# Column sums of a modulation row: seven of twelve made by TensorE transpositions and VectorE row sums

## The reference, cut to what matters

```python
def modulation(cond, w, b, n):
    m = jax.nn.silu(cond) @ w[:, :n * D_MODEL] + b[:n * D_MODEL]
    return jnp.split(m, n, axis=-1)
...
sh, sc, gt = modulation(c_lat, w_ada[i], b_ada[i], 3)
u = x * (1.0 + sc) + sh
```

## Time and profile before

| | us |
|---|---|
| median of 3 runs (lowest, highest) | 1789.02 (1788.63, 1791.81) |
| the profiled execution's own time | 1790.88 |
| its span, first to last instruction | 1789.1 |
| mean granted TensorE clock, share of full speed | 0.990 |
| TensorE matmul busy | 1737.5 |
| VectorE busy | 1334.8 |
| ScalarE busy | 903.4 |

### The profile page before, as it was taken

How to read it: one execution, slowest core, us unless ns; L and a number is a source line. 1 busy time by engine, 2 the same in 40 slices (tenths; PEclk the granted TensorE clock), 3 DMA queues, 4 the chain that set the end, 5 groups by cost and what they waited for, 6 DMA issues and landing times.

```text
span 1789.1 us, 22330 instructions
## 1 busy us (share of the span) xinstructions
PE 1737.5 (97%) x8112; PEld 1396.1 (78%) x8112; DVE 1334.8 (75%) x1779; ACT 903.4 (50%) x1366; POOL 142.2 (8%) x202
## 2 busy tenths in 40 slices
PE   7999999999999999999999999999989989999997
PEld 6887887788877777888677778787767768777885
DVE  6967777868777777687876767788676878766766
ACT  7446563455456644464653456555633355443432
POOL 1100000001100000011111100000101101110000
PEclk9999999999999999999999999999999999999999
DMA  8955454558845544679877843333748879876563
GB/s 294 323 190 187 167 165 142 184 181 285 273 155 163 176 141 143 252 275 377 273 249 235 298 176 120 129 117 120 273 165 324 298 267 316 285 252 226 199 215 118
DMA packets 110406, 390.36 MB, mean 218 GB/s; under 512 B 16200, under 2 KB 16864, under 8 KB 108736
## 3 DMA queue, kind: packets, MB, share of 16 engines
q1 hardware_dynamic: 74672, 268.99, 42.6%
q0 software_dynamic: 27856, 101.19, 18.3%
q10 hardware_dynamic: 7776, 18.82, 2.8%
HBM read 384.75 MB, written 4.19 MB: 217 GB/s over the span
## 4 chain that ended last, share of the span: by engine, by line
PE 79%; DVE 11%; DMA 4%; ACT 3%; issue 3%; ACTq 0%; DVEq 0%; SPq 0%
PE L L329 22%; PE L L331 21%; PE L L330 21%; DVE wl L282 3%; PE TP L433 3%; DMA stage<-in_w_stream 2%; DVE macc L596 1%; DMA mstage<-in_w_mod 1%; PE AB L1872 1%; PE AB L1800 1%; ACT wh L261 1%; PE AB L1877 1%; PE AB L1876 1%; PE TP L1886 1%; PE AB L2102 1%
## 5 line engine op out<-in xcount | busy, mean ns | idle before, releaser
L329 PE MATMUL L<-wh,xth 128*128 128x512 f32 x1952 | 797.2, 408 | 15.2 <-DVE wl L282 8.6
L282 DVE TENSOR_TENSOR wl<-stage,wh 128x1024 fp32r<-128x1024 f32 x504 | 613.4, 1221 | 249.6 <-ACT wh L261 248.8
L261 ACT ACTIVATE wh<-stage 128x1024 fp32r<-128x1024 f32 x504 | 531.1, 1057 | 521.8 <-PE L L331 377.8
L331 PE MATMUL L<-wh,xtl 128*128 128x512 f32 x1952 | 767.5, 393 | 0.0
L330 PE MATMUL L<-wl,xth 128*128 128x512 f32 x1952 | 765.6, 392 | 0.0
L329 PEld LDWEIGHTS L<-wh,xth 128*128 128x128 f32 x1952 | 370.1, 190 | 113.3 <-issue 22.7
L331 PEld LDWEIGHTS L<-wh,xtl 128*128 128x128 f32 x1952 | 369.3, 189 | 80.9
L330 PEld LDWEIGHTS L<-wl,xth 128*128 128x128 f32 x1952 | 370.6, 190 | 75.3 <-issue 4.8
L596 DVE SCALAR_TENSOR_TENSOR macc<-mstage,scols,macc 128x1024 f32<-128x1024 f32 x240 | 306.9, 1279 | 11.3 <-DMA mstage<-in_w_mod 11.0
L625 POOL DMA_DIRECT2D mstage<-in_w_mod x192 | 139.2, 725 | 1499.0 <-DVE macc L596 1031.5
L1174 DVE SCALAR_TENSOR_TENSOR pa<-tab,AB 128x384 f32<-128x384 f32 x48 | 26.6, 555 | 65.3 <-PE AB L1872 35.1
(11 more groups left out here) (205 smaller groups left out, 1332.4 us busy)
## 6 DMA issues: line engine op xcount, KB each, us to landing
stage<-in_w_stream SPq DMA_DIRECT2D x504, 512.0 KB, 4.5
mstage<-in_w_mod POOLq DMA_DIRECT2D x192, 512.0 KB, 6.0
X<-in_x SPq DMA_DIRECT2D x4, 512.0 KB, 8.0
arena<-in_ctx ACTq DMA_DIRECT2D x1, 2048.0 KB, 14.2
x_kept<-X ACTq DMA_DIRECT2D x1, 2048.0 KB, 10.6
X<-x_kept ACTq DMA_DIRECT2D x1, 2048.0 KB, 8.3
arena<-in_b_ada ACTq DMA_DIRECT2D x2, 1024.0 KB, 10.6
arena<-in_ln_g ACTq DMA_DIRECT2D x2, 1024.0 KB, 9.0
```

What stands on the lines that cost most here:

```text
L261: nc.scalar.activation(wh[:, s % SPLITS].rearrange("p a b -> p (a b)"), stage[:, s % RING, :], ACT.Copy).then_inc(hi_ready, 1)
L282: nc.vector.tensor_tensor(wl[:, s % SPLITS].rearrange("p a b -> p (a b)"), stage[:, s % RING, :], wh[:, s % SPLITS].rearrange("p a b -> p ...
L329: nc.tensor.matmul(o, xh, w[0], start=start, stop=False, skip_group_check=True)
L331: last = nc.tensor.matmul(o, xl, w[0], start=False, stop=True, skip_group_check=True)
```

## The change

Seven of the twelve sums (i = 1 in both layers, two each, and i = 4, 5 and 6) are made in another way. TensorE transposes the eight pieces of `macc` into turning banks (`turn_sums`), four to a bank, so one sum takes two uses. VectorE sums each bank along its rows (`sum_turned`, 128 x 4 x 128 to 128 x 4) into a new small buffer `msum`, which frees the bank, and adds the bias as before (`mod_columns_turned`), now from `msum`; it raises `mod_summed` itself. The four uses per layer, named ("ms", l, j), stand in TURNS ahead of the next layer's x turns. In the layers, TensorE makes them in two groups of two uses behind slots 3 and 5 (before: all behind slot 5), and VectorE reads them in its steps 4 and 6, and adds the bias in step 6 (before: step 8). The sum for i = 4 stands behind slot 23 (before: 25) and its wait for `r_sb` falls away; VectorE's part is in its step 26 (before: 30). The sum for i = 5 stays, with its wait for `z_min` moved behind the loop. Waits for `mod_cols` in TensorE's list fall away. The counters of the uses are moved on in ScalarE's and TensorE's lists. The other five sums stay as they are.

```diff
-    return t + [("yb", l, 3)] + [("x", l + 1, m) for m in range(4)]
+    return t + [("yb", l, 3)] + [("ms", l, j) for j in range(4)] + [("x", l + 1, m) for m in range(4)]
...
+        msum = sb("msum", [P, 2, 8])
...
+        def flat_bank(m):
+            return TP[(m - 1) % 2].rearrange("p a b -> p (a b)")
...
+        def sum_turned(dve, m, w, j):
+            dve.wait_ge(tp_ready, m)
+            nc.vector.tensor_reduce(msum[:, w, 4 * j:4 * j + 4], flat_bank(m).rearrange("p (c k) -> p c k", c=4), AX.X, ALU.add)\
+                .then_inc(bank_free(m), 1)
+
+        def mod_columns_turned(dve, c, scale, targets, uses):
+            for m in uses:
+                turned(dve, m)
+            for w, which, layer in targets:
+                nc.vector.scalar_tensor_tensor(out=mcols[:, which, at(c, 8)], in0=msum[:, w, :],
+                                               scalar=1.0 if scale else 0.0,
+                                               in1=bcols[:, layer].rearrange("p a b -> p (a b)")[:, at(c, 8)],
+                                               op0=ALU.add, op1=ALU.add).then_inc(mod_cols, 1)
+            dve.sem_inc(mod_summed, 1)
...
(ScalarE)
+            u.n += 2
             evac_ctx = evac_to(0, 2048, 1024)
...
                     turned(act, u.n)
+                    u.n += 4
...
(VectorE, layer end)
-                    if n == 8:
-                        mod_columns(dve, 2 * l + 1, 8 * l + KT, True, [(0, 1, 0), (1, 0, 0)])
+                    if n in (4, 6):
+                        for j in range(2):
+                            sum_turned(dve, TURN["ms", l, n - 4 + j], n // 2 - 2, j)
+                    if n == 6:
+                        mod_columns_turned(dve, 8 * l + KT, True, [(0, 1, 0), (1, 0, 0)], [TURN["ms", l, j] for j in range(4)])
...
+            def mod_columns_block2(w, c, scale, which):
+                uses = [u.take()[1] for _ in range(2)]
+                for j, m in enumerate(uses):
+                    sum_turned(dve, m, w, j)
+                mod_columns_turned(dve, c, scale, [(w, which, 1)], uses)
...
+                if n == 26:
+                    mod_columns_block2(0, KT, True, 2)
                 if n >= 28:
                     turn_scaled(n - 28)
                 mod_ctx(n - 4)
-                if n == 30:
-                    mod_columns(dve, 4, KT, True, [(0, 2, 1)])
...
-            mod_columns(dve, 5, KT + 8, True, [(1, 2, 1)])
+            mod_columns_block2(1, KT + 8, True, 2)
...
-            mod_columns(dve, 6, 0, False, [(0, 2, 1)])
+            mod_columns_block2(0, 0, False, 2)
...
(TensorE)
+            def turn_sums(m, w, j):
+                turned(pe, m - 2)
+                for b in range(4):
+                    a = COLS * j + P * b
+                    last = nc.tensor.transpose(flat_bank(m)[:, P * b:P * b + P], macc[:, w, a:a + P], ident[:])
+                last.then_inc(tp_ready, 1)
+
+            def turn_sums_block2(i, w):
+                pe.wait_ge(mod_sum, mod_done(0, i + 1))
+                for j in range(2):
+                    turn_sums(u.take()[1], w, j)
...
-                    if n == 5:
-                        modulation_columns(l, 1, (0, 1))
+                    if n in (3, 5):
+                        pe.wait_ge(mod_sum, mod_done(l, 2))
+                        for j in range(2):
+                            turn_sums(TURN["ms", l, n - 3 + j], n // 2 - 1, j)
...
-                if p == 25:
-                    pe.wait_ge(once("r_sb"), 1)
-                    modulation_columns(0, 4, (0,))
+                if p == 23:
+                    turn_sums_block2(4, 0)
...
-                turned(pe, len(TURNS) + m + 1)
+                turned(pe, len(TURNS) + 2 + m + 1)
...
                 if m == 11:
-                    pe.wait_ge(once("z_min"), 8)
-                    modulation_columns(0, 5, (1,))
-            pe.wait_ge(mod_cols, MOD_COLS[6])
+                    turn_sums_block2(5, 1)
+            pe.wait_ge(once("z_min"), 8)
...
             low_rank_ready(2)
-            modulation_columns(0, 6, (0,))
-            pe.wait_ge(mod_cols, MOD_COLS[7])
+            turn_sums_block2(6, 0)
```

## The result

| | before | after |
|---|---|---|
| median of 6 runs, us | 1789.39 | 1779.07 |
| lowest, highest, us | 1786.98, 1792.29 | 1776.22, 1782.63 |
| ratio after to before, 95% interval | | 0.9931 [0.9914, 0.9947] |
| profiled execution: time, span, us | 1790.88, 1789.1 | 1779.59, 1777.8 |
| its mean granted clock | 0.990 | 0.995 |

Faster by 0.7%: 12.3 us by the ratio, 10.3 by the medians, where 6.9 were forecast. The sign was right and the size was not: the new median lies just inside the range, but the ratio on the median that the forecast started from is 0.9931 x 1789.02 = 1776.7, under the range's low end of 1778.3. The interval of the ratio makes 1773.6 to 1779.5 of it, so the time is well under the forecast of 1782.1, while the end of the range is inside the noise.

A forecast was written before the change was run, and what follows sets the result against it. TensorE, busy for 97% of the span, was taken to bound the kernel, with column sums costing their time and the clock behind them. Gains of 1.3 + 2.3 + 0.9 + 0.9 + 1.5 = 6.9 us gave 1782.1 us, range 1778.3 to 1787.5.

The forecast's parts named there:

- The direct terms: Layer ends: waits 2.15 and 2.17 us, eight transpositions 0.79, reductions 0.65; context sums: no wait, 0.9 us gained each.
- the bank wait: Layer 1's end: the x turn behind slot 6 waits 0.6 us for VectorE to free the third transposed group's bank.
- The sum ahead of the heads: The sum for i = 6: gain 1.5 us, kept near the lower bound of 0.7, where the clock falls all the same.
- the forecast's own bound of 3.5: Ahead of the heads: upper bound of the gain, 3.5 us, with full clock and VectorE's operation holding TensorE until 1049.2.
- The base of the forecast: Whole kernel: starting time 1789.02 us, the median of the runs, 1.9 below the profiled 1790.88.
- Sum: Whole kernel: 1.3 + 2.3 + 0.9 + 0.9 + 1.5 = 6.9 us gained, giving 1782.1 us.
- (c): Whole kernel: TensorE comes earlier to places where it waits anyway, gain halved to 1785.6 us; chance 0.15.
- The layer ends: Ends of layers 0 and 1: transpositions in place of column sums gain 1.3 and 2.3 us.
- The clock in the new waits: Layer ends: no clock fall behind TensorE's 2.15 us idle and 0.8 us of transpositions, judged from the wait of 2.70.
- (b): Clock holds everywhere, ahead of the heads too, and layer 1's second wait is hidden: 9.5 us gained, 1779.5; chance 0.13.
- (a): Layer ends: the clock falls behind the new waits, leaving 0.5 to 3.7 us gained, 1785.3 to 1788.5; chance 0.18.
- (d): Layer ends: TensorE's turns wait for reductions behind late weight splits, with a fallen clock; slower, about 1793 us; chance 0.06.

The follow-up runs named there:

- the three parts: Kernel before with only the layer ends changed, only the sum ahead of the heads, or only i = 4 and 5: 0.9990, 0.9968, 0.9994 to the kernel before.

## Why the prediction was right in most of its steps and wrong in its size

- **The direct terms held.** Waits of 1.95 for 2.15 and 2.17; the bank wait 0.34 for 0.6; reductions of 0.682 for 0.65; eight transpositions 0.80 for 0.79; no wait at the context sums. In the profiled executions layer 0 gave 1.28 for 1.3, and layer 1 with the context sums 3.9 for 4.1.
- **The step that failed** is in "The sum ahead of the heads": "There is still a stretch of 4.7 us ... with no wide matmul in it, longer than the 3.63 us behind which the clock fell, so I keep near the lower bound: 1.5 us". It measured 3.2 to 3.8 us in the profiled executions and 5.9 on average (3.0 to 8.4), because the clock no longer fell there. Whether wide matmuls stand in such a stretch is not what decides. Transpositions did not bring the clock down, as the 6.9 us of nothing else showed, and one-column matmuls in their place did. That this is the reason at this place too is drawn from those runs and from 0 falls in 9 profiles against 5 in 5: no run kept the one-column sum and only shortened it or took away the wait behind it. And the kernel before had the clock low there for 6.8 to 10.2 us in every profile, of which the forecast's own bound of 3.5 knew only the shortest case.
- **The base of the forecast** was some 2 to 3 us too low. The "Sum" carried the difference of 1.9 us between the profiled time and the median of three runs over whole, and rival (c) took it as a sign that others lose less to the clock than the profiled one. It was the noise of three runs: on three other chips the medians are 1791.9, 1791.2 and 1792.0, and the profiled execution lost less than the average (0.990 against 0.988). At the places that change it was no exception, though: low stretches of 17.1 us in all (3.4, 6.8 and 6.8), and in the two other profiles with the sums as before at all three of them 17.1 and 20.5. So this error moved the forecast time, and does not explain why the gain was larger.
- **The layer ends** came out at 1.8 on average for 3.6; the interval holds the forecast, so that they were taken too high isn't shown. Two things point that way: the profile read had low stretches of 10.2 us there, four profiles 8.5 on average, and the fall behind the new wait in 2 of 8 was taken at nothing.
- **The clock in the new waits** was taken to hold, from one profile of the earlier trace rows. It held in 12 of 14 such waits (all six in layer 0, six of eight in layer 1). But the row did not bear the inference: the clock fell behind that very wait in 8 of 13 profiles. That this step came out nearly right was luck.
- **The rivals.** (b) was nearest in size, and by mechanism it is what happened at the heads; the second wait in layer 1 was not hidden (0.34 us). (a) happened in 2 of 8 profiles in layer 1 and in none in layer 0. (d) did not happen here, but is real: 4.32 us in the kernel with one slot less of slack. (c) did not.

Open: whether the three parts add up to the whole (9.1 and 11.0 us), what the wait of 1.95 us in layer 0 costs by itself, and which part of the change ahead of the heads (other instructions, less of them, or no wait for the columns) keeps the clock up.

## What to carry to other kernels

Read the granted clock behind every group of narrow matmuls: behind 3.6 us of one-column matmuls in a row it was low in 22 of 30 cases here, and the shorter of these stretches (3.4 us) cost 1.6 us, the longer twice that. Setting them apart by wide matmuls won it back, and making them transpositions did too. Where the clock falls depends on the execution; take its mean over many runs, for it is a term of the sum with a spread of its own (most of 13 us here). One profile gives one draw, and a wait that it passes at full clock may fall in the next. Before moving a producer earlier or a reader later, count the slots of slack in the bank between them: here one slot less turned a wait of 2 us into one of 4.3 and a fallen clock.

## What the runs showed of the hardware that was not expected

- 64 float32 transpositions in a row (6.9 us) left the granted clock at 1.00 at two places of one profile; 64 records of one column at the same places had it at 0.50 for 10.2 and 13.6 us, and behind them wide matmuls of 512 columns did not bring it back at once (it stayed low for 4.0 us behind the first group).
- At waits of TensorE the clock fell in some executions and not in others: in 2 of 14 at some 1.94 us with transpositions behind them, in 9 of 13 at 2.54 us, in 7 and 8 of 13 at the two of 2.70 us. The wait of 2.70 us in the earlier trace rows was passed at full clock in that profile, and the one of 2.54 us at 1247 wasn't in the kernel after.
- Executions of one and the same kernel differ by 13 us, and most of it goes with the clock (-1.55 us per 0.001, correlation -0.91).
